# Constant products in TensorE's waits at four stage boundaries of each layer

## The reference

```
h = rmsnorm(x);  p = h @ w_in                       # one wide projection, split into 11 parts
o_dn = gated delta rule, forwards + backwards       # 4 heads of 128, chunks
o_hg = HGRN2 scan, forwards + backwards             # 4 heads of 128, chunks
merged = sigmoid(gate_dn) * (o_dn @ w_branch_dn) + sigmoid(gate_hg) * (o_hg @ w_branch_hg)
x = x + merged @ w_out
x = x + conv_ffn(rmsnorm(x))                        # width 2816
```

## Time and profile before

| | us |
|---|---|
| median of three executions | 2867.22 |
| lowest, highest | 2864.11, 2872.46 |
| the profiled execution's own time | 2869.75 |
| its span, first to last instruction | 2868.0 |

### The profile page before, as it was taken

How to read it: one execution, slowest core, us unless ns; L and a number is a source line. 1 busy time by engine, 2 the same in 40 slices (tenths; PEclk the granted TensorE clock), 3 DMA queues, 4 the chain that set the end, 5 groups by cost and what they waited for, 6 DMA issues and landing times. The chain is left out here.

```text
span 2868.0 us, 48673 instructions
## 1 busy us (share of the span) xinstructions
PE 2744.2 (96%) x20562; PEld 2243.7 (78%) x20562; DVE 1511.0 (53%) x2273; ACT 1195.7 (42%) x1933; POOL 848.6 (30%) x476
## 2 busy tenths in 40 slices
PE   8989998999999999899989999999999999999999
PEld 6777876888888877778768888888787778888887
DVE  7555577347626465655763575264786553531120
ACT  5553665233213245546652332222444543342331
POOL 2343020024544423430200244444002224344433
PEclk9989998999999999899999999999999999999999
DMA  5102202333423331022033333233422213333322
GB/s 174 59 4 73 74 3 81 105 110 96 117 74 99 100 89 59 4 80 67 3 97 97 108 96 110 81 104 87 114 79 71 72 56 106 90 97 97 99 81 81
DMA packets 414586, 236.32 MB, mean 82 GB/s; under 512 B 24244, under 2 KB 404770, under 8 KB 413730
## 3 DMA queue, kind: packets, MB, share of 16 engines
q1 hardware_dynamic: 413490, 233.18, 28.2%
q10 hardware_dynamic: 880, 0.02, 0.0%
HBM read 226.88 MB, written 6.29 MB: 81 GB/s over the span
## 5 line engine op out<-in xcount | busy, mean ns | idle before, releaser
L2380 POOL TENSOR_TENSOR WLO<-RAW,WHI 128x1024 fp32r<-128x1024 f32 (+1 forms) x199 | 523.1, 2635 | 972.7 <-ACT WHI L2216 972.7
L146 PE MATMUL PS<-HHI,WHI 128*128 128x512 f32 x2016 | 796.6, 395 | 4.8 <-DVE WLO L3112 2.2
L148 PE MATMUL PS<-HHI,WLO 128*128 128x512 f32 x2016 | 787.6, 391 | 0.0
L147 PE MATMUL PS<-HLO,WHI 128*128 128x512 f32 x2016 | 787.3, 391 | 0.0
L146 PEld LDWEIGHTS PS<-HHI,WHI 128*128 128x128 f32 x2016 | 380.5, 189 | 97.0 <-issue 7.4
L147 PEld LDWEIGHTS PS<-HLO,WHI 128*128 128x128 f32 x2016 | 380.6, 189 | 81.1 <-issue 3.1
L148 PEld LDWEIGHTS PS<-HHI,WLO 128*128 128x128 f32 x2016 | 380.0, 188 | 79.8
L2216 ACT CAST WHI<-RAW 128x1024 fp32r<-128x1024 f32 (+1 forms) x202 | 221.6, 1101 | 509.3 <-PE PS L148 496.3
L2369 DVE TENSOR_TENSOR X<-X,PS 128x512 f32<-128x512 f32 x48 | 32.9, 688 | 334.1 <-PE PS L148 334.1
L3174 POOL TENSOR_TENSOR WLO<-RAW,WHI 128x1280 fp32r<-128x1280 f32 x31 | 91.3, 2948 | 319.1 <-ACT WHI L3057 319.1
L2352 DVE SCALAR_TENSOR_TENSOR ACC<-GP,PARS,ACC 128x512 f32<-128x512 f32 x88 | 163.1, 1853 | 3.1
(11 more groups left out here) (501 smaller groups left out, 4783.0 us busy)
## 6 DMA issues: line engine op xcount, KB each, us to landing
RAW<-in_w_up SPq DMA_DIRECT2D x88, 512.0 KB, 3.8
RAW<-in_w_mlp SPq DMA_DIRECT2D x64, 512.0 KB, 3.8
RAW<-in_w_in SPq DMA_DIRECT2D x46, 512.0 KB, 4.0
RAW<-in_w_down SPq DMA_DIRECT2D x32, 704.0 KB, 4.5
RAW<-in_w_in SPq DMA_DIRECT2D x20, 1024.0 KB, 5.2
RAW<-in_w_gate SPq DMA_DIRECT2D x32, 512.0 KB, 4.1
RAWQ<-in_w_in SPq DMA_DIRECT2D x24, 512.0 KB, 3.9
RAW<-in_w_out SPq DMA_DIRECT2D x24, 512.0 KB, 4.5
```

Source lines behind the costliest of these rows:

```text
L146: e.matmul(out, wh, xh, start=first and n == 0, stop=False)
L147: e.matmul(out, wh, xl, start=False, stop=False)
L148: last = e.matmul(out, wl, xh, start=False, stop=final and n == len(quads) - 1)
L2380: pool.tensor_tensor(slot(WLO, u), source(u), slot(WHI, u), ALU.subtract).then_inc(lo_s, 1)
```

## The change

A helper multiplies the constant tile of ones with the first `n` constant tiles, in plain float32, into a part of PSUM that nothing holds at that time. Nothing reads the result. With n = 2 the product has 128 rows, 128 weight columns and 256 moving columns. Fifteen of them are added in each of the two layers: 2 at the end of TensorE's list of the delta stage, 3 ahead of the first wait of the projection stage, 5 in the first preparation of the HGRN stage (2 before the turned keys, 2 before the suffix sums, 1 before the exponents), and 5 ahead of the first wait of the branch stage. `prepare(0)` is written out with them between its two halves; its own instructions and their waits stay in their order.

```diff
+def idle_product(pe, out, C, n):
+
+    pe.matmul(out, C[:, ONES, :], C[:, 0:n, :].rearrange("p a n -> p (a n)"), start=True, stop=True)
@@ delta_stage, end of TensorE's list
                         if levels:
                             state(j, 1)
+                for _ in range(2):
+                    idle_product(pe, bank(0, 0)[:, 0:2 * P], C, 2)
@@ hgrn_proj_stage, start of TensorE's list
+                for _ in range(3):
+                    idle_product(pe, PS[:, 7, 0:2 * P], C, 2)
                 for g in range(3):
@@ hgrn_stage
-                prepare(0)
+                for _ in range(2):
+                    idle_product(pe, PS[:, 7, 0:2 * P], C, 2)
+                for d in lanes:
+                    turned_keys(0, d)
+                for _ in range(2):
+                    idle_product(pe, PS[:, 7, 0:2 * P], C, 2)
+                for d in lanes:
+                    suffix(0, d)
+                idle_product(pe, PS[:, 7, 0:2 * P], C, 2)
                 exponents(0, 0, 0)
@@ branch_stage, start of TensorE's list
+                for _ in range(5):
+                    idle_product(pe, PS[:, 0, 0:2 * P], C, 2)
                 for c in range(4):
                     pe.wait_ge(sq_s, c + 1)
```

## The result

The kernel after takes **2870.47 us** (median of 20 executions, 2866.35 to 2875.74) against 2867.35 us before (20 executions, 2858.76 to 2872.46): ratio 1.0017, 95% interval 1.0011 to 1.0023. It is slower by 3 to 4 us, where 2865 us and a small gain were forecast. The time lies inside the range and inside the 0.3% in which one measurement tells nothing from no change, but twenty executions of each do tell it. The profiled execution took 2871.25 us (span 2869.5 us).

A forecast was written before the change was run, and what follows sets the result against it. TensorE was taken as the bound, busy 96% of the span and mostly at full clock. Terms summing to −2.8 us gave 2867.0 us from the profiled execution or 2864.4 us from the median; forecast 2865 us, range 2858.5 to 2871.5 us.

The forecast's parts named there:

- Price of a product: On TensorE, 256 columns cost 0.22 us, so a product 0.44 us at full clock, 0.86 us at 1.2 GHz.
- Delta's end: Two products at the delta stage's end finish 0.15 us after VectorE's last addition, costing 0.1 us per layer.
- Projection's start: Three products before the projection's first wait cost nothing; with delta's two they keep the clock up, gaining 1.5 us per layer.
- A wait that takes it back: Sign of a wrong forecast: a wait in the projection stage that cancels the 3.0 us gained there.
- HGRN's start: Five products delay VectorE's first scaling 0.5 us, costing 0.35 us per layer; 0.7 us gained in the first layer.
- Branch's start: Five products end 0.1 us late in TensorE's wait, counted as 0; bounds 0.8 us gain, 0.1 us loss per layer.
- the sum itself: Whole kernel: −2.8 us (delta and projection), +0.7 − 0.7 (HGRN), 0 (branch), together −2.8 us.
- only moved: Low-clock stretches move into the scans, which swing either way by more than the gain: 2867.2 us; chance 0.22.
- The products meet the low clock: Products run at 1.2 GHz at the branch and HGRN starts, both layers: +4.8 us, 2872 us; chance 0.11.
- More is won: Other executions lose time at branch starts and elsewhere, so the gain is 6.6 us and above: 2860.6 us or less; chance 0.09.

The follow-up runs named there:

- hgrn_first_two: Kernel before plus only the two products ahead of the turned keys in the HGRN stage, both layers: 2867.33 us, ratio 1.0004.
- no_products: Kernel before again as a control, all fifteen products left out but `prepare(0)` kept written out: 2869.83 us, ratio 1.0006.
- pad_ten: Kernel before plus ten tiny 32x32 products in the first projection's dense run, both layers, none of the change's own: 2875.77 us, ratio 1.0031.
- tiny_all: The change with all fifteen products shrunk to 32x32 corners, same instructions and next to no work: 2874.23 us, ratio 1.0024 against before.
- pad_seventy_four: Kernel before plus 74 tiny 32x32 products in the first projection's dense run, both layers: 2879.22 us, ratio 1.0049.
- only_hgrn: Kernel before plus only the five full products in the HGRN stage, both layers: 2872.69 us, ratio 1.0017.
- tiny_hgrn: Kernel before plus only the five HGRN products, each shrunk to a 32x32 corner, both layers: 2871.85 us, ratio 1.0012.
- only_projection: Kernel before plus only the two products at delta's end and three at the projection's start, both layers: 2868.75 us, ratio 1.0002.
- only_branch: Kernel before plus only the five products at the branch stage's start, both layers: 2869.35 us, ratio 1.001.
- without_hgrn: The change without its five HGRN products, the ten others at full work: 2866.30 us, ratio 0.9994 against before; run again, 2866.05 us, 0.9998.
- wide_without_hgrn: The change without its HGRN products, the same columns in fewer, wider products, 24 instructions per layer for 40: 2865.49 us, ratio 0.9993 against before.
- tiny_without_hgrn: The change without its HGRN products, the ten others shrunk to 32x32 corners: 2865.70 us, ratio 0.9998 against before.

## Why the prediction was wrong

**Price of a product: right.** Ten matmuls of 256 columns take 2.40 us from first start to last end, 0.22 us apart; 0.44 us a product was forecast.

**Delta's end: right.** The products end 0.14 us after VectorE's last addition (0.15 forecast) and the next stage begins 0.39 us after it, 0.28 us before: 0.1 us a layer.

**Projection's start: right at its place.** The first product starts 1.49 us after the stage's start as before, the clock stays at 1.00, and the stages last 115.0 us for 116.6 us: 1.6 us a layer (1.5 forecast). A wait that takes it back isn't there. But before doesn't lose this each time: in the fifteen profiles without these products at full work (before among them) the clock fell at 22 of the 30 projection starts, in the five with them at none of ten. That makes 2.4 us on average for both layers, not 3.0.

**HGRN's start: the delay right, its price open.** The first scaling is 0.44 us late (0.5 forecast). At the end of the first chunk 0.2 us less than before are left, but that point lies anywhere from 30.1 to 32.6 us after the stage's start in kernels without these products, so two executions can't tell whether the delay lives on. `hgrn_first_two`, which makes this delay, is at +0.7 us with a standard error of 0.9. The gain of 0.7 us for the low clock behind the first layer's start was a single execution's: without these products at full work the clock fell at 8 of 32 HGRN starts, with them at none of eight.

**Branch's start: right in this execution, its bound mis-sized.** 0.1 us late, stage unchanged at 143.9 us. A fall there costs 2.3 us (0.8 forecast), so these products are an insurance worth more than the prediction gave them. A fall, whole or half, came at 17 of 30 branch starts in the fifteen profiles without these products at full work (at both in `no_products`, `hgrn_first_two`, `pad_ten` and two more), and at none of ten with them. The stages without them are 1.1 us longer on average, 2.2 us for both layers.

**The step that failed is the sum itself**, which took the terms of the four places for the whole change, and with it the three HGRN products and the ones before them at "cost nothing" because a wait covers them. `tiny_all` puts it at +6.3 us for the whole change's list, and the difference to the change, 2 us (standard error 1.5), is what shows of the local gains. Nearly all the loss hangs on the five of the HGRN stage (+4.6 us alone, with or without work); the change without them is at −1.5 us (standard error 0.8, so no gain is shown). In the profiles the second delta stage is 122.8 to 125.3 us in all five kernels that hold the last three HGRN products, and 119.2 to 121.6 us in thirteen of the other fifteen (`pad_ten` and `pad_seventy_four` being the two). The count alone doesn't set that length, though: `only_hgrn`, `tiny_hgrn`, `only_projection` and `only_branch` all have 20 instructions more ahead of it, and it lasts 125.3, 124.7, 120.9 and 121.6 us, with the clock low for 34, 31, 24 and 24 us.

The clock that was won locally isn't all lost again elsewhere, as the change alone would suggest (mean granted clock 0.9817, as in the 138 executions of before in the five groups). Without the HGRN five it is 0.9828, 0.9834 and 0.9829 in `without_hgrn`, its repetition and `wide_without_hgrn`, and 0.9823 in `tiny_without_hgrn`, which has the list of the first two without the work.

The rivals: **only moved** came nearest, with the right place (the scans) and the right balance (the mean clock over the executions is the same, though the falls at the boundaries are gone), but it was to be without a sign, and the loss has one and a cause. **The products meet the low clock** had the sign and was wrong: they ran at 1.00 at each of the boundaries shown. **More is won** has no run for its time, but its premise was right: the falls at the branch start that one execution missed are there in others.

What stays open: how a stall becomes lost time. Over the twenty profiles the length of the four scans together (444.3 to 457.2 us) is fitted by 415.2 + 0.53 × the stalls (all waits put down to "issue", 20.6 to 29.4 us) + 0.30 × the time at the low clock in them (65 to 92 us), with 86% of the variance; the standard errors are 0.19 and 0.05. Between before and after that makes +2.5 us by stalls and +1.0 us by the clock out of 6.0 us. But stalls and low clock go together (correlation 0.6), and `hgrn_first_two` has 24.7 us of stalls and shows no loss. Whether stalls bring the clock down, or only meet it, no run here separates. And the first delta stage of after, longer by 2.8 us with the list of before ahead of it, looks like chance between executions: with the same list up to its last products it was 123.8 us in `only_hgrn`, and with the same two products at its end 125.3 us in `without_hgrn`.

## What to carry to other kernels

Before pricing an instruction in a wait at nothing, ask what it does to the list behind it: in long runs of small matmuls the engine stood still at multiples of 256 instructions, and moving those places cost more here (from nothing to about 7 us) than the clock won at the projection's start (3.2 us in the profile). To tell such an effect from the change's own, run the change with its work shrunk to nothing and its instructions kept, and the kernel before with a few idle instructions somewhere harmless. A change of 0.1% that can't be told from the second of these isn't a finding about the change.
